# Layer 0's experts: three experts in two blocks of 128 slots, and weight buffers given out by last use

## The reference, cut to what matters

```
pg = softmax(h @ wg + bg); gi = argmax(pg)            # one of 4 groups of 8 experts
tw, ti = top_k(softmax(logits of that group), 2)      # two experts in it
expert = gi * 8 + ti
# for every expert e, over the tokens that chose it:
gate, up = split(h_rows @ w_gu[e], 2)                 # 1024 x 1024
y_rows   = (silu(gate) * up) @ w_down[e]              # 512 x 1024
```

## Time and profile before

| | |
|---|---|
| median of 3 runs | 2883.3 us (2883.15 to 2885.7) |
| the profiled execution's own time | 2889.0 us |
| its span in the profile | 2887.2 us |
| mean granted TensorE clock | 0.964 of full |
| TensorE busy | 2695.0 us, 93% |
| experts of layer 0, on TensorE | 992.6 to 1639.7 us |
| experts of layer 1, on TensorE | 2268.3 to 2831.5 us |

### The profile page before, as it was taken

The page is one execution under the profiler, slowest core; times in us unless marked ns, Lnnn a source line. Parts: engine busy times, 40 slices in busy tenths (PEclk is TensorE's granted clock), DMA queues, the critical chain, the costliest instruction groups (busy, mean ns, idle before and its releaser), DMA issues.

```text
span 2887.2 us, 31132 instructions
## 1 busy us (share of the span) xinstructions
PE 2695.0 (93%) x12000; PEld 1410.1 (49%) x12000; DVE 1080.5 (37%) x2459; ACT 554.0 (19%) x1149; POOL 250.8 (9%) x356
## 2 busy tenths in 40 slices
PE   5999999999989799999999699899999799999992
PEld 3444456557645444444444354477755444444440
DVE  3322337008546522222222272277756411111115
ACT  2211111128611100000000030178821000000002
POOL 0010200002011100000000000000011000000002
PEclk8999999999999799999999899999999799999996
DMA  9663111114140399999999630120030799999995
GB/s 358 218 244 91 34 41 47 45 23 92 63 174 30 127 356 331 384 371 333 399 357 344 238 130 30 25 41 2 2 134 30 246 385 404 403 404 400 403 406 209
DMA packets 225597, 602.76 MB, mean 209 GB/s; under 512 B 17608, under 2 KB 20896, under 8 KB 216872
## 3 DMA queue, kind: packets, MB, share of 16 engines
q1 hardware_dynamic: 210184, 545.15, 52.4%
q0 software_dynamic: 15264, 55.58, 4.9%
HBM read 556.55 MB, written 44.41 MB: 208 GB/s over the span
## 4 chain that ended last, share of the span: by engine, by line
PE 82%; DMA 7%; SPq 4%; DVE 4%; issue 1%; ACT 0%; POOL 0%; POOLq 0%; DVEq 0%; ACTq 0%
PE PS L1715 26%; PE PS L804 22%; PE PS L1334 8%; PE PS L1718 7%; DMA ar<-in_expert_w_gu_dram 4%; PE PS L1154 4%; PE PS L1166 4%; PE PS L1177 4%; SPq L1709 3%; PE PS L1723 1%; PE PS L496 1%; PE PS L1353 1%; DVE ar L2098 1%; PE PS L692 1%; PE PS L1728 1%
## 5 line engine op out<-in xcount | busy, mean ns | idle before, releaser
L1715 PE MATMUL PS<-ar 128*128 128x512 f32 x2016 | 883.1, 596 | 4.1 <-DVE ar L1900 2.6
L804 PE MATMUL PS<-ar 128*128 128x512 f32 (+1 forms) x1600 | 674.4, 578 | 0.0
L1715 PEld LDWEIGHTS PS<-ar 128*128 128x128 f32 x2016 | 379.6, 191 | 475.6 <-issue 470.4
L804 PEld LDWEIGHTS PS<-ar 128*128 128x128 f32 x1600 | 299.2, 190 | 330.7 <-issue 325.8
L1334 PE MATMUL PS<-ar 128*128 128x512 f32 x576 | 257.2, 601 | 0.6 <-DVEq L335 0.6
L1718 PE MATMUL PS<-ar 128*64 128x512 f32 x1056 | 239.8, 607 | 15.5 <-DMA ar<-in_expert_w_gu_dram 14.0
L1837 ACT ACTIVATE ar<-PS 128x512 f32<-128x512 f32 x53 | 31.6, 597 | 1151.1 <-PE PS L1715 914.0
L1208 DVE CUSTOM_DVE_ANT_0 ar<-PS,ar 128x640 f32<-128x640 f32 (+2 forms) x208 | 158.0, 797 | 203.6 <-POOL ar L1124 133.5
L1930 DVE TENSOR_TENSOR ar<-PS,ar 128x1024 f32<-128x1024 f32 x53 | 64.9, 1225 | 296.4 <-issue 137.0
L1334 PEld LDWEIGHTS PS<-ar 128*128 128x128 f32 x576 | 108.0, 192 | 124.6 <-issue 123.8
L1263 ACT ACTIVATE ar<-ar 128x641 f32<-128x641 f32 (+4 forms) x208 | 159.5, 772 | 0.8 <-DVE ar L1208 0.8
(11 more groups left out here) (229 smaller groups left out, 1926.6 us busy)
## 6 DMA issues: line engine op xcount, KB each, us to landing
ar<-in_expert_w_gu_dram SPq DMA_DIRECT2D x128, 2048.0 KB, 17.9
ar<-in_expert_w_down_dram SPq DMA_DIRECT2D x64, 2048.0 KB, 17.9
ar<-in_ada_w_dram SPq DMA_DIRECT2D x24, 2048.0 KB, 13.6
ar<-yd SPq DMA_DIRECT2D x36, 512.0 KB, 6.6
ar<-in_ab_w_in_dram SPq DMA_DIRECT2D x7, 2048.0 KB, 9.4
h2d<-ar SPq DMA_DIRECT2D x18, 512.0 KB, 2.6
ar<-in_swa_w_in_dram SPq DMA_DIRECT2D x3, 2048.0 KB, 10.4
ar<-mod SPq DMA_DIRECT2D x3, 1536.0 KB, 8.0
```

What stands on the lines that cost most here:

```text
L804: mm = nc.tensor.matmul(out_, lhs, rhs, start=(k == 0), stop=(k == KC - 1))
L1715: return nc.tensor.matmul(out, lhsT, ws[0][:, k, cols], start=start, stop=stop)
```

## The change

`PAIRS = (3, 8)` becomes three settings by layer, `PAIRS, SHARED, MAINS = (0,8),(6,0),(2,0)`. Layer 1 keeps its 8 pairs. Layer 0 has no pairs; it has six groups of three experts in two blocks. In each of the two blocks a main expert has slots 0 to 95 and the third expert of the group has slots 96 to 127, so the third has 32 slots in each of both blocks, 64 in all. By rank: 0 and 1 whole blocks, 2 to 7 the thirds, 8 to 19 the mains, 20 to 31 whole blocks. That makes 2 + 12 + 12 = 26 blocks in layer 0, in the order: 2 whole, group, then 2, 2, 3, 2 and 3 whole blocks, each followed by a group.

A group's third expert has its three pieces loaded once and used by both blocks. So its buffers are held longer than those of the mains, and the ring is replaced: each piece takes the buffer whose content is used up first, by the order of TensorE's products, and waits for the last block that uses that content. There are still six buffers and 96 pieces.

`block_product` now makes a matmul for each part of the block; a part of 96 slots is made as one of 64 and one of 32. A step in a shared block is thus three matmuls, with 64, 32 and 32 columns of weights, each by 512.

The router's small work changes with it: `route_shift` has one matmul for each main (two in layer 0, to partitions 96 to 127), `route_slots` copies the lists in other slices, and `route_rest` computes each expert's slots with a sum over the ranks' borders. The diff, cut to its core:

```diff
-PAIRS = (3, 8)
+PAIRS, SHARED, MAINS = (0,8),(6,0),(2,0)
+def rank_bounds(l):
+    pairs, shared, mains = PAIRS[l], SHARED[l], MAINS[l]
+    a = 2 + 2 * pairs
+    return a, a + shared, a + shared + shared * mains
+def rank_short(l):
+    a, b, c = rank_bounds(l)
+    short = [0, 64, P - 32 * MAINS[l], 32, 0]
+    return [(at, short[i] - short[i + 1]) for i, at in enumerate((2, a, b, c)) if short[i] != short[i + 1]]
+def moe_blocks(l):
+    pairs, shared, mains = PAIRS[l], SHARED[l], MAINS[l]
+    a, b, c = rank_bounds(l)
+    whole = lambda r, col: dict(parts=[(r, 0, P)], col=col)
+    first = [whole(0, 0), whole(1, 1)]
+    groups = [[dict(parts=[(2 + 2 * i, 0, 64), (3 + 2 * i, 64, P)], col=2 + i)] for i in range(pairs)]
+    groups += [[dict(parts=[(b + mains * i + j, 0, 96), (a + i, 96, P)], col=2 + pairs + mains * i + j) for j in range(mains)]
+               for i in range(shared)]
+    rest = [whole(r, 2 + pairs + shared * mains + r - c) for r in range(c, EXP)]
+    seq = first + groups[0]
+    for i in range(1, len(groups)):
+        seq += rest[(i - 1) * len(rest) // (len(groups) - 1):i * len(rest) // (len(groups) - 1)] + groups[i]
+    return seq
...
+                for b in range(nb + 1):
+                    for part, k in (("g", b), ("u", b), ("d", b - 1)):
...
+                        for r, lo, hi in self.blocks[k]["parts"]:
+                            if (part, r) not in known:
+                                known[part, r] = len(self.pieces)
+                                self.pieces.append(dict(part=part, rank=r))
+                            i = known[part, r]
+                            self.pieces[i]["last"] = k
+                            self.at.setdefault((part, k), []).append((i, lo, hi))
...
+                    return dict(g=4 * x["last"], u=4 * x["last"] + 1, d=4 * x["last"] + 6)[x["part"]]
+                for i, x in enumerate(self.pieces):
+                    q = min(range(6), key=lambda q: (free_at(q), q))
+                    self.fills[q] += 1
+                    x.update(buf=q, fill=self.fills[q], freed=held[q])
+                    held[q] = i
...
         def route_shift(pe, l):
...
-            nc.tensor.matmul(PS[64:128, 7, 0:n], cst[:, C_ID:C_ID + 64], Vp[:, 2:2 + n], start=True, stop=True).then_inc(S(f"r{l}_shift"), 1)
+            for j in range(MAINS[l]):
+                mm = nc.tensor.matmul(PS[96:128, 7, 64 + j * (b - a):64 + (j + 1) * (b - a)], cst[:, C_ID + 32 * j:C_ID + 32 * j + 32],
+                                      Vp[:, a:b], start=True, stop=True)
...
-                ch(V.tensor_scalar(t1, rank, 1.5, None, ALU.is_gt))
-                ch(V.scalar_tensor_tensor(out=t1, in0=rank, scalar=2 * np_ + 1.5, in1=t1, op0=ALU.is_lt, op1=ALU.mult))
-                V.tensor_scalar(cap, t1, -64.0, float(P), ALU.mult, ALU.add)
-                ch(V.scalar_tensor_tensor(out=t1, in0=t1, scalar=64.0, in1=cnt, op0=ALU.mult, op1=ALU.add))
+            for i, (at, less) in enumerate(rank_short(l)):
+                to = t2 if i else t1
+                ch(V.tensor_scalar(to, rank, at - 0.5, float(less), ALU.is_lt, ALU.mult))
+                if i:
+                    ch(V.tensor_tensor(t1, t1, t2, ALU.add))
+            V.tensor_scalar(cap, t1, -1.0, float(P), ALU.mult, ALU.add)
+            ch(V.tensor_tensor(t1, t1, cnt, ALU.add))
...
         def block_product(out, lhsT, ws, k, cols, start, stop):
-            if len(ws) == 1:
-                return nc.tensor.matmul(out, lhsT, ws[0][:, k, cols], start=start, stop=stop)
-            for h in range(2):
-                half = slice(64 * h, 64 * h + 64)
-                mm = nc.tensor.matmul(out[half], lhsT[:, half], ws[h][:, k, cols], start=start, stop=stop)
+            for w, lo, hi in ws:
+                for at, to in (((lo, hi),) if hi - lo != 96 else ((lo, lo + 64), (lo + 64, hi))):
+                    mm = nc.tensor.matmul(out[at:to], lhsT[:, at:to], w[:, k, cols], start=start, stop=stop)
             return mm
```

More of the change, by code:

```diff
@@ L284, in program, with __init__, free_at, buf @@
         share(("{}_wx",), "r0", "r1", 2)
-        n_blk = [EXP - PAIRS[l] for l in range(2)]
+        class Moe:
+            def __init__(self, l):
+                self.l, self.n = l, f"m{l}"
+                self.blocks, self.pieces, self.at, self.fills = moe_blocks(l), [], {}, [0] * 6
+                nb, known = len(self.blocks), {}
+                for b in range(nb + 1):
+                    for part, k in (("g", b), ("u", b), ("d", b - 1)):
+                        if not 0 <= k < nb:
+                            continue
+                        for r, lo, hi in self.blocks[k]["parts"]:
[5 more added lines that the diff above has]
+                            self.at.setdefault((part, k), []).append((i, lo, hi))
+                held = [None] * 6
+                def free_at(q):
+                    if held[q] is None:
+                        return -1
+                    x = self.pieces[held[q]]
+                    return dict(g=4 * x["last"], u=4 * x["last"] + 1, d=4 * x["last"] + 6)[x["part"]]
[4 more added lines that the diff above has]
+                    held[q] = i
+                assert len(self.pieces) == 3 * EXP
+            def buf(self, i):
+                return R(piece_at[self.pieces[i]["buf"]], 4096)
+            def load(self, sp, i):
+                x = self.pieces[i]
+                if x["freed"] is not None:
+                    f = self.pieces[x["freed"]]
+                    sp.wait_ge(*done(f"{self.n}_" + dict(g="ga", u="gu", d="dn")[f["part"]], f["last"] + 1))
+                r = x["rank"]
+                e = r if r < 2 else sp.value_load(ord_i[0:1, r:r + 1], min_val=0, max_val=EXP - 1)
+                weight_load(sp, self.l, x["part"], e, self.buf(i)).then_inc(S(f"{self.n}_w{x['buf']}"), 16)
+            def weights(self, pe, part, b):
+                k = 4 if part == "d" else KC
+                for i, lo, hi in self.at[part, b]:
+                    pe.wait_ge(*done(f"{self.n}_w{self.pieces[i]['buf']}", 16 * self.pieces[i]["fill"]))
+                return [(self.buf(i).rearrange("p (k n) -> p k n", k=k), lo, hi) for i, lo, hi in self.at[part, b]]
@@ L287, in program @@
+        n_blk = [len(moe_blocks(l)) for l in range(2)]
         share(("{}_tr", "{}_hbT", "{}_ga", "{}_gu", "{}_silu", "{}_mul", "{}_gt", "{}_guT", "{}_dn", "{}_y"), "m0", "m1", n_blk[0])
-        share(tuple(f"{{}}_w{q}" for q in range(6)), "m0", "m1", 256)
+        for q in range(6):
+            share((f"{{}}_w{q}",), "m0", "m1", 16 * Moe(0).fills[q])
         for q in range(2):
@@ L1552, in route_first @@
         def route_first(dve, l):
-            n, np_ = f"r{l}", PAIRS[l]
+            n = f"r{l}"
             ch = chain(dve)
@@ L1563, in route_first @@
             ch(V.tensor_copy(cnt, PS[:, 5, 64:64 + EXP]))
-            if np_ == 0:
-                return
             ch(V.scalar_tensor_tensor(out=key, in0=cnt, scalar=float(EXP), in1=cst[:, C_KEY:C_KEY + EXP], op0=ALU.mult, op1=ALU.add))
@@ L1574, in route_order @@
         def route_order(dve, l):
-            if PAIRS[l] == 0:
-                return
             ch = chain(dve)
@@ L1583, in route_shift @@
         def route_shift(pe, l):
-            if PAIRS[l] == 0:
-                return
+            a, b, c = rank_bounds(l)
             pe.wait_ge(*done(f"r{l}_perm", 1))
-            n = 2 * PAIRS[l]
-            nc.tensor.matmul(PS[64:128, 7, 0:n], cst[:, C_ID:C_ID + 64], Vp[:, 2:2 + n], start=True, stop=True).then_inc(S(f"r{l}_shift"), 1)
+            if PAIRS[l]:
+                mm = nc.tensor.matmul(PS[64:128, 7, 0:a - 2], cst[:, C_ID:C_ID + 64], Vp[:, 2:a], start=True, stop=True)
+            for j in range(MAINS[l]):
+                mm = nc.tensor.matmul(PS[96:128, 7, 64 + j * (b - a):64 + (j + 1) * (b - a)], cst[:, C_ID + 32 * j:C_ID + 32 * j + 32],
+                                      Vp[:, a:b], start=True, stop=True)
@@ L1590, in route_slots @@
+            mm.then_inc(S(f"r{l}_shift"), 1)
         def route_slots(dve, l):
-            n, np_ = f"r{l}", PAIRS[l]
+            n, np_, ns, m = f"r{l}", PAIRS[l], SHARED[l], MAINS[l]
+            a, b, c = rank_bounds(l)
+            at, nb = 2 + np_, n_blk[l]
             ch = chain(dve)
             V = nc.vector
-            if np_ == 0:
-                slot_places(dve, ch, idxE[:, EXP:2 * EXP], src_i, dst_i, key, EXP, 0).then_inc(S(f"{n}_idx"), 1)
-                return
             dve.wait_ge(*done(f"{n}_perm", 1))
@@ L1599, in route_slots @@
             V.tensor_copy(Vb[:, 0:2], Vp[:, 0:2])
-            V.tensor_copy(Vb[:, np_ + 2:EXP - np_], Vp[:, 2 * np_ + 2:EXP])
+            V.tensor_copy(Vb[:, at + ns * m:nb], Vp[:, c:EXP])
             two = lambda a: a.rearrange("p (i h) -> p i h", h=2)
-            V.tensor_copy(Vb[0:64, 2:2 + np_], two(Vp[0:64, 2:2 + 2 * np_])[:, :, 0])
+            if np_:
+                V.tensor_copy(Vb[0:64, 2:at], two(Vp[0:64, 2:a])[:, :, 0])
+            if ns:
```

(31 more changed lines are left out.)

## The result

The changed kernel takes 3147.1 us (median of 4 runs, 3143.8 to 3149.6) against 2884.3 us of the kernel before on the same chip: a ratio of 1.091 with a 95% interval of 1.089 to 1.093, 263 us more. The forecast of 2825 us had the wrong sign. Rival 1, two tile widths that exclude each other, had given 3159 us.

A forecast was written before the change was run, and what follows sets the result against it. TensorE's block count was taken to bound layer 0's expert stage: 640.3 - 581.7 - 0.3 = 58 us less, carried to the 2883.3 us median, gives 2825 us; range 2815 to 3165, the forecast's own 2815 to 2845.

The forecast's parts named there:

- Rival 1: Layer 0's shared blocks: 64- and 32-column tiles exclude each other, 2.02 us a step, 276 us slower, 3159 us; chance 0.38.
- part 2: Cost of a three-tile step in layer 0's shared blocks: between 0.86 and 2.02 us, taken as no dearer than a full step.
- the lower end: Layer 0's shared steps: disjoint 64- and 32-column tiles run together, so a step costs nothing beyond a full one's 0.86 us.
- The milder form of rival 1: Layer 0's shared steps: widths take turns without a price for the change, 1.72 us a step, 3073 us; chance 0.06.
- Part 1: Layer 0's expert stage on TensorE: 26 blocks instead of 29, 640.3 us down to 581.7, a saving of 58.6.
- The switches: Tiled runs standing alone between full-width ones in layer 0's six groups: 1.75 us a group, 10.5 us in all.
- Overflow: End of layer 0's experts: no overflow block ran before, and by the routing counts no more work appears.
- Part 3: Layer 0's weight loads: 220 MB need 548 us at 402 GB/s, covered by TensorE's work; cost nothing, bound 0 to 15 us.
- Part 4: Small router work of layer 0: 0.6 us more on VectorE, covered by idle time, and at most 0.3 us of TensorE.

The follow-up runs named there:

- e1: The changed kernel with the main expert's 96 slots cut into three 32-column tiles instead of 64 + 32; 2825.3 us, 0.980 of the kernel before.
- e2: The changed kernel with each product running all its 64-column steps first, then all its 32-column ones; 3078.8 us, 1.067 of the kernel before.
- e6: The changed kernel with three groups instead of six in layer 0, tiles still 64 + 32 + 32; 3047.1 us, 1.057 of the kernel before.
- e3: The changed kernel with shared blocks at full width for the main expert alone, third experts' products left out, their weights still loaded; 2818.0 us.
- e4: e1 with the old ring (piece i in buffer i mod 6) in place of buffers by last use; 2900.9 us, 1.006 of the kernel before.
- e8: e1 with the third expert's pieces loaded anew for the second block, 114 pieces in layer 0 instead of 96; 2900.5 us.
- e5: The changed kernel with settings turned back to 3 pair blocks and no groups in layer 0, its other new code kept; 2885.3 us, ratio 1.0005.

## Why the prediction was wrong

**The step that failed is part 2**, "I take the lower end". The bounds of that step, 0.86 and 2.02 us, were both worked out, and the measured step is 1.99 us. All changes seen in the trace before were between a full-width matmul and a tile inside it, as the prediction says; what it concluded from that, that disjoint tiles of two widths would run together for nothing, did not hold: a 64-column tile and a disjoint 32-column tile take turns too, and each change costs (the starts in the change's trace; e1, e2, e6). The price of a change from the kernel before, 0.52 and 0.49 us in place of 0.43, fitted disjoint tiles as well: 0.14 to 0.15 us for a change and its second slot, against 0.136 in e2. Rows 6 and 7 showed two tiles of one width, and four tiles of one width. "Tiles run side by side" was read out of them; "tiles of one width run side by side" is what they said.

Rival 1 was right in mechanism and size: 24 steps x 1.16 us x 12 blocks less 58 gave 276 us, measured 263. In parts: taking turns about 244 us and the 72 changes left about 10 us (e2 against e1, 253.5), the other 504 changes 68.3 us (the change against e2), less e1's gain of 59. The milder form of rival 1, turns without a price for the change, had 3073 us; the change's own steps and e2 rule it out.

The Trainium skill ("TensorEngine Tiling (Array Packing)", Tiling Modes, Key Properties) says that a change of tiling mode drains the engine. The trace agrees, as far as starts can show it: at each change the loads stand idle 0.81 to 0.84 us, and the next width starts 0.53 us after the last matmul of the other.

**Part 1** was right once the width was one: 26 blocks gave 2825.3 us in e1, forecast 2825. e1's stage on TensorE ran from 988.7 to 1576.4 us, 587.7, where 589 was forecast. The switches were over-sized, 7.3 us measured (e3) for 10.5. That e1 hits 2825 to the microsecond is partly luck: e3, without switches, is 66.0 us under the kernel before, where the same sum gives 640.3 - 571.2 = 69.1. The two errors of 3 us, each about as large as the spread of the runs, cancel. **Overflow**: no matmul beyond the 26 blocks' own in layer 0, 14 x 48 = 672 full ones.

**Part 3** was right at the pace that part 1 needs: in e1 TensorE waits 0.2 us for weights between 1020 and 1570 us, and the DMAs move 392 GB/s (1100 to 1560 us). SyncE's wait for buffers, forecast at 100 to 200 us, was 329.6 us, so the slack was larger than forecast. The prediction had also read the waits of the kernel before by one row of two: 425.3 us are those that full-width products end, and 45.8 us more end with half-width ones, 471.1 in all; in layer 1 it is 88.6 and 87.2, 175.8 in all. The order of the two stages stays the same. That buffers by last use were needed was argued and is now shown by e4, and that the third's pieces had to be kept, by e8. **Part 4** was right as far as it can be seen: in the changed kernel VectorE still stands idle for 1.03 us between `route_rest` and the copy behind it, against 1.70 before, so the longer router work is covered; e5 shows no difference; and after the last down product TensorE's gap is 20.6 us in the changed kernel and 20.0 in e1 against 21.4.

**The chances.** The rule against the change, the break at each change of width in the earlier trace rows, and the lack of any row with two narrow widths together were all named, and rival 1 still got less than the forecast. Four tiles of 32 columns had been shown by rows to cost nothing; 64 + 32 + 32 had not. A split that needs the unseen case, where a seen one does the same work, should have had the lower chance.

## What to carry to other kernels

In all rows of this case (float32, operands of 128 rows) column tiles of TensorE run side by side when they have the same width, and take turns when they don't. So cut every part of a step to the narrowest width in it: four matmuls of 32 columns by 512 cost what one of 128 does. Other types and shorter matmuls were not tried with two widths. If two widths can't be avoided, sort the work by width, but expect each width to cost its own full pass. Before taking a row as proof of concurrency, ask what is equal in that row and not in the change. And when weights are kept over several blocks, give buffers out by last use: a ring made the queue wait behind the one buffer still in use, and in e4 nine of the thirteen waits then also cost clock.

## What the runs showed that was not expected

The queue's order cost almost one and a half times what its waits were: in e4 a wait of 4.55 us was followed by 5 us at half clock, in all 22.5 us beside 52.0 of waiting. And a float32 step in four 32-column tiles came at the price of a full-width step to within 1% (0.440 against 0.442 us), with the weight loads of the next four tiles hidden behind the matmuls.
